# State chain of the recurrent heads: 64-column matmuls, one per head, in place of 128x128 products

## The chip, the cores and the metric

The kernel runs on one core of a Trainium2 chip. The metric is the device time of one execution in microseconds (us); lower is better. Times are given as the median of several runs. A core has TensorE (matmuls and weight loads), VectorE, ScalarE, GpSimd and SyncE (DMA issue), each with its own instruction queue; they meet at semaphores.

## The reference

One decoder layer over 512 tokens with 16 learned meta tokens ahead of them (528 in all), width 2048. After an RMS norm one projection feeds two groups of heads: 16 recurrent heads of 64 (RWKV-7) and 8 differential-attention heads. Both are gated, concatenated, projected, normed and added to the input. The change is in the recurrent heads:

```python
def step(S, inp):
    r_t, w_t, k_t, v_t, kk_t, b_t = inp
    sa = jnp.einsum('bhvk,bhk->bhv', S, -kk_t)
    S = S * w_t[:, :, None, :] + sa[..., None] * b_t[:, :, None, :] + v_t[..., None] * k_t[:, :, None, :]
    y = jnp.einsum('bhvk,bhk->bhv', S, r_t)
    return S, y
```

Each head carries a state S of 64x64 through all tokens; y is normed per head, a bonus term is added, and it is gated.

## The kernel before

The kernel is written engine by engine, with semaphores by hand. Two recurrent heads fill the 128 partitions and are called a pair; there are 8 pairs. The tokens are padded to 576 and cut into 9 chunks of 64 (`NC`), in 3 groups of 3 (`GC`, `NG`). The program runs through iterations: in iteration i TensorE computes the projection tiles of one pair or attention head (`feature_tile`, L547: three products of the split f32 operands for every 128 input features, 264 moving columns twice or 512 once), and between these matmuls it puts the work of the pair before. What stands where is a table of places by hand: each part of the work is a generator that yields the place of its next step, and `upto` runs the steps that are due between two projection matmuls. Nothing of the order is decided at run time; each engine's queue is fixed.

For each group `inv_pe` forms the triangular matrices of the three chunks (L646, by row halves, one matmul per head with 64 rows), inverts them in f16 (L667 to L701), and `chain_pe` then goes through the chunks one by one. With a chunk's two heads in one 128x128 array it makes five f32 products:

- g (L723): the chunk's keys times `home`, which holds on its diagonal quarters the two heads' states, and the values on the others. `home` is a 128x128 tile of `suv`, one for each chunk.
- first part of y (L725), from the same `home` with the queries; not in chunk 0.
- u (L728): the inverse `t_t` times g, once VectorE has copied g into `g_sb` (L1523). VectorE (L1528) and ScalarE (L1081) put the upper and the lower head's u into `home`.
- s (L733): the new state from `bk_tok` and `home`; not in the last chunk. VectorE scales it and adds the decayed old state that ScalarE prepared (L1538, L1075).
- second part of y (L736): from `home` and the masked matrix `b_in`; not in chunk 0. ScalarE copies y of a group to `ysum` (L1088).

So with 8 pairs there are 72 products g, 72 u, 64 s and 64 of each part of y, 336 in all. Products g, u and s use the PSUM columns 0 to 127 of `mb`, y those from 512 on. Of the blocks that g, u, s and the second y put out only the diagonal or a half is used: where the two heads' data lie side by side, the operands hold zeros or the result of the other quarters is left unread. The f32 matmul is executed in two passes, so the trace has two matmul and two weight-load records for each.

Other lines named below: L588, L592, L616 norms of the recurrent heads; L788 and L790 the product of attention with the values, where L790 has only the 16 rows of the meta tokens; L780 and L782 its transposes, L782 with 16 columns; L1055, L1059, L1062 ScalarE's and L1499 VectorE's copies in the inversion.

Of the kernel before, what the change touches and what calls it, by code (L numbers as in the profile page):

```python
# [34 lines left out]
P = 128  # L35
# [88 lines left out]
def hybrid_layer(nc, x, meta_tokens, pre_norm_w, w_in, rwkv_mu, rwkv_w0, rwkv_w_up, rwkv_a0, rwkv_a_up,  # L124
# [3 lines left out]
    with ctx:  # L128
# [40 lines left out]
        def carve(stage, name, n, dt=F32):  # L169
            at = taken.get(stage, 0)  # L170
            words = n if dt is F32 else n // 2
            taken[stage] = at + words
            assert taken[stage] <= ARENA, (stage, name, taken[stage])
            v = arena[:, at:at + words]
            return v if dt is F32 else v.bitcast(dt)
# [26 lines left out]
        b_in3 = [v.rearrange("p (c t) -> p c t", c=GC) for v in b_in]  # L202
        b_in5 = [v.rearrange("p (c k h t) -> p c k h t", c=GC, k=2, h=2) for v in b_in]
        state0 = carve("rwkv", "state0", HD)
        g_sb = carve("rwkv", "g_sb", P)
        top, bottom = slice(0, HD), slice(HD, P)
        halves = (top, bottom)

# [325 lines left out]
        def _(pe):  # L534
# [169 lines left out]
            def chain_pe(i, g, late, work, gn):  # L704
                b = g % 2
                n = groups_so_far(i, g, late)
                for c in range(GC):
                    ch = g * GC + c
                    m = chunks_so_far(i, ch, late)
                    home = suv[:, chunk_home(i, ch, late), :]  # L710
                    yield chain_at(g, 3 * c, late, work)
                    if c == 0:
                        pe.wait_ge(s("inv_taken"), n)
                        pe.wait_ge(s("k_masked"), 2 * n)
                        if g == 0:
                            pe.wait_ge(s("state_zeroed"), i)
                    if ch > 0:
                        pe.wait_ge(s("s_taken"), states_so_far(i, ch - 1, late))
                        if g > 0 and c == 0:
                            pe.wait_ge(s("y_taken"), n - 1)  # L720
                    o = mb[:, 0:P]
                    yo = mb[:, 512 + c * P:512 + (c + 1) * P]
                    mm(o, ar3[:, ch, 0:P], home, start=True, stop=True).then_inc(s("g_done"), 1)  # L723
                    if ch > 0:
                        mm(yo, home, ar3[:, ch, P:2 * P], start=True, stop=False)  # L725
                    yield chain_at(g, 3 * c + 1, late, work)
                    pe.wait_ge(s("g_taken"), m)
                    mm(o, t_t[b][:, c * P:(c + 1) * P], g_sb, start=True, stop=True).then_inc(s("u_done"), 1)  # L728
                    yield chain_at(g, 3 * c + 2, late, work)
                    pe.wait_ge(s("u_taken"), m)  # L730
                    pe.wait_ge(s("u_lower_taken"), m)
                    if ch < SC:
                        mm(o, bk_tok[g][:, c * P:(c + 1) * P], home, start=True,  # L733
                           stop=True).then_inc(s("s_done"), 1)
                    if ch > 0:
                        last = mm(yo, home, b_in3[g][:, c, P:2 * P], start=False, stop=True)  # L736
                        if c == GC - 1:
                            last.then_inc(s("y_done"), 1)

# [137 lines left out]
        def _(act):  # L877
# [186 lines left out]
            def chain_act(i, g, late, work, gn):  # L1064
                n = groups_so_far(i, g, late)
                for c in range(GC):
                    ch = g * GC + c
                    home = suv[:, chunk_home(i, ch, late), :]
                    yield chain_at(g, 3 * c + 0.3, late, work)
                    if 0 < ch < SC:  # L1070
                        act.wait_ge(s("s_taken"), states_so_far(i, ch - 1, late))
                        if ch == 1:
                            act.wait_ge(s("ends_made"), i - late)
                        for h, rows in enumerate(halves):
                            last = A(state0[rows, :], home[rows, rows], ACT.Copy, scale=w_end_of(i, late)[rows, ch:ch + 1])  # L1075
                        last.then_inc(s("s_scaled"), 1)
                    yield chain_at(g, 3 * c + 1.3, late, work)
                    if 0 < ch < SC:
                        act.wait_ge(s("s_scaled"), kept_so_far(i, ch, late))
                    act.wait_ge(s("u_done"), chunks_so_far(i, ch, late))  # L1080
                    A(home[bottom, bottom], mb[bottom, bottom], ACT.Copy).then_inc(s("u_lower_taken"), 1)  # L1081
                yield chain_at(g, 8.4, late, work)
                act.wait_ge(s("y_done"), n)
                c0 = 1 if g == 0 else 0
                lo, w = (g * GC + c0 - 1) * CH, (GC - c0) * CH
                y4 = mb[:, 512:512 + GC * P].rearrange("p (c h t) -> p c h t", c=GC, h=2)
                for h, rows in enumerate(halves):
                    last = A(ysum[rows, lo:lo + w].rearrange("p (c t) -> p c t", t=CH), y4[rows, c0:, h, :], ACT.Copy)  # L1088
                last.then_inc(s("y_taken"), 1)

            def attn_act(i, gn):
                n = i - NP_
# [143 lines left out]
        def _(dve):  # L1236
# [279 lines left out]
            def chain_dve(i, g, late, work, gn):  # L1516
                for c in range(GC):
                    ch = g * GC + c
                    m = chunks_so_far(i, ch, late)
                    home = suv[:, chunk_home(i, ch, late), :]  # L1520
                    yield chain_at(g, 3 * c + 0.3, late, work)
                    dve.wait_ge(s("g_done"), m)
                    V.tensor_copy(g_sb, mb[:, 0:P]).then_inc(s("g_taken"), 1)  # L1523
                    yield chain_at(g, 3 * c + 1.3, late, work)
                    dve.wait_ge(s("u_done"), m)
                    if 0 < ch < SC:
                        dve.wait_ge(s("s_scaled"), kept_so_far(i, ch, late))
                    V.tensor_copy(home[top, top], mb[top, top]).then_inc(s("u_taken"), 1)  # L1528
                    if ch < SC:
                        yield chain_at(g, 3 * c + 2.3, late, work)  # L1530
                        dve.wait_ge(s("s_done"), states_so_far(i, ch, late))
                        if ch == 0:
                            dve.wait_ge(s("ends_made"), i - late)
                        for rows in halves:
                            dst = suv[rows, chunk_home(i, ch + 1, late), rows]
                            src, w = mb[rows, rows], w_end_of(i, late)[rows, ch:ch + 1]
                            if ch:
                                ins = STT(dst, src, w, state0[rows, :], ALU.mult, ALU.add)  # L1538
                            else:
                                ins = TS(dst, src, w, None, ALU.mult)  # L1540
                        ins.then_inc(s("s_taken"), 1)
# [156 lines left out]
```

## Time and profile before

| what | us |
|---|---|
| median of 3 runs | 1394.71 |
| lowest and highest run | 1393.51 and 1394.75 |
| the profiled execution, its time | 1395.48 |
| the profiled execution, its span | 1393.7 |
| TensorE matmuls busy | 1329.2 |
| TensorE weight loads busy | 1136.1 |
| VectorE busy | 731.8 |
| ScalarE busy | 673.1 |
| GpSimd busy | 304.8 |

The profile lists busy time by engine: PE are TensorE's matmuls, PEld its weight loads, which overlap matmuls; DVE is VectorE, ACT ScalarE and POOL GpSimd. The time of a matmul runs from its start to its modelled end; matmuls are pipelined, so several are in flight and their durations add up to more than the time they take from the queue. That is read from one start to the next. The timeline view gives start and length in us, and merges instructions of the same line and shape that follow each other (x2 and so on); its first number plus its second is the end of the last of them. The waits view tells for how long an engine sat idle and which instruction let it go on.

### The profile page before, as it was taken

What the parts mean: (1) busy time and instruction counts of PE and PEld (TensorE: products, weight loads), DVE (VectorE), ACT (ScalarE), POOL (GpSimd) and SP (SyncE); (2) the same over time, 40 slices, a digit from 0 to 9 for tenths busy, and PEclk for the clock granted to TensorE, in tenths of its full rate; (3) what the DMA queues carried; (4) which work ended last, traced back from release to release, by engine and by line L of the source; (5) the groups of instructions that cost most, each with busy time, mean ns of one, the idle gap of its engine ahead of it and who ended that gap; (6) DMA issues with size and microseconds to landing.
All of it is one profiled execution on the core that took longest, in us unless ns stands there. A gap on an engine that the chain in (4) does not pass through costs nothing.

```text
span 1393.7 us, 24026 instructions
## 1 busy us (share of the span) xinstructions
PE 1329.2 (95%) x9393; PEld 1136.1 (82%) x9393; DVE 731.8 (53%) x1653; ACT 673.1 (48%) x1550; POOL 304.8 (22%) x234
## 2 busy tenths in 40 slices
PE   3999999999999999999999999999999999989997
PEld 3988888797888879889788877898888988768885
DVE  5346767767677686866866433433343333530013
ACT  4435656556565555656555544444443444432331
POOL 3330001000000100001000323333334333334544
PEclk9999999999999999999999998999999999999998
DMA  6221121111112111111112222222222222235333
GB/s 211 71 76 56 47 63 40 56 54 47 56 46 63 47 54 51 51 56 47 53 47 61 83 63 61 71 81 71 75 76 76 69 76 76 67 92 203 109 93 141
DMA packets 151264, 102.24 MB, mean 73 GB/s; under 512 B 6398, under 2 KB 140640, under 8 KB 149600
## 3 DMA queue, kind: packets, MB, share of 16 engines
q1 hardware_dynamic: 151152, 100.71, 24.3%
q8 instruction: 75, 1.23, 0.4%
q14 instruction: 37, 0.30, 0.1%
HBM read 96.49 MB, written 4.19 MB: 72 GB/s over the span
## 4 chain that ended last, share of the span: by engine, by line
PE 83%; DVE 9%; ACT 4%; issue 3%; POOL 1%; DMA 0%; DVEq 0%; ACTq 0%; SPq 0%
PE tile L547 48%; PE tile L807 2%; PE tile L808 2%; PE tile L809 2%; PE ma L773 2%; PE ma L646 2%; PE ma L686 1%; PE ma L679 1%; PE mb L788 1%; PE ma L667 1%; DVE arena L1499 1%; PE mb L790 1%; PE ma L809 1%; PE mb L807 1%; PE ma L807 1%
## 5 line engine op out<-in xcount | busy, mean ns | idle before, releaser
L547 PE MATMUL tile<-hn_hi,w_hi 128*128 128x264 f32 (+1 forms) x1696 | 446.6, 326 | 0.3
L547 PE MATMUL tile<-hn_hi,w_lo 128*128 128x264 f32 (+1 forms) x1696 | 438.6, 322 | 2.2 <-ACT arena L1062 2.2
L547 PE MATMUL tile<-hn_lo,w_hi 128*128 128x264 f32 (+1 forms) x1696 | 437.8, 321 | 0.0
L885 ACT CAST w_hi<-w_raw 128x512 fp32r<-128x512 f32 x324 | 200.4, 619 | 365.3 <-PE tile L547 254.9
L1177 POOL TENSOR_TENSOR w_lo<-w_raw,w_hi 128x512 fp32r<-128x512 f32 x196 | 255.1, 1302 | 448.3 <-ACT w_hi L885 448.2
L547 PEld LDWEIGHTS tile<-hn_hi,w_hi 128*128 128x128 f32 x1696 | 276.5, 190 | 29.2 <-issue 10.2
L547 PEld LDWEIGHTS tile<-hn_hi,w_lo 128*128 128x128 f32 x1696 | 276.3, 190 | 18.8 <-ACT arena L1062 3.6
L547 PEld LDWEIGHTS tile<-hn_lo,w_hi 128*128 128x128 f32 x1696 | 276.2, 190 | 11.6 <-issue 2.2
L1192 POOL TENSOR_TENSOR arena<-arena,power 128x10 f32<-128x10 f32 (+3 forms) x28 | 43.9, 1569 | 620.3 <-DVE arena L1356 471.2
L1499 DVE TENSOR_TENSOR arena<-ma,c 128x384 f16<-128x384 f32 x120 | 66.7, 556 | 45.9 <-PE ma L667 44.6
L1436 DVE TENSOR_TENSOR w_lo<-w_raw,w_hi 128x512 fp32r<-128x512 f32 x128 | 87.5, 683 | 1.3
L1059 ACT ACTIVATE arena<-ma 128x384 f16<-128x384 f32 x120 | 58.8, 490 | 46.3 <-PE ma L679 45.0
L1599 DVE TENSOR_SCALAR arena<-mb,arena 128x128 f32<-128x128 f32 x32 | 11.2, 350 | 91.9 <-PE mb L790 91.9
L807 PE MATMUL tile<-w_hi,hn_hi 128*128 128x512 f32 x128 | 53.1, 415 | 5.5 <-DVE hn_lo L1618 5.5
L1062 ACT ACTIVATE arena<-ma 128x384 f16<-128x384 f32 x120 | 58.3, 486 | 0.0
L808 PE MATMUL tile<-w_lo,hn_hi 128*128 128x512 f32 x128 | 51.6, 403 | 0.0
L809 PE MATMUL tile<-w_hi,hn_lo 128*128 128x512 f32 x128 | 51.5, 403 | 0.0
L1483 DVE TENSOR_TENSOR arena<-arena,c 128x384 f16<-128x384 f16 x144 | 49.0, 350 | 0.8
L1587 DVE TENSOR_TENSOR ma<-ma,c 128x128 f32<-128x128 f32 x32 | 9.6, 299 | 75.1 <-PE mb L773 75.1
L679 PE MATMUL ma<-arena 128*128 128x128 f16 x360 | 41.7, 224 | 3.3 <-DVE arena L1499 2.0
L667 PE MATMUL ma<-arena 128*128 128x128 f16 x360 | 41.6, 224 | 3.2 <-ACT arena L1059 3.1
L1075 ACT ACTIVATE arena<-arena 64x64 f32<-64x64 f32 x112 | 38.5, 344 | 12.0 <-DVE arena L1538 11.2
(262 smaller groups left out, 2090.1 us busy)
## 6 DMA issues: line engine op xcount, KB each, us to landing
w_raw<-w_in SPq DMA_DIRECT2D x260, 256.0 KB, 2.8
w_raw<-w_out SPq DMA_DIRECT2D x64, 256.0 KB, 3.0
big<-x SPq DMA_DIRECT2D x4, 1024.0 KB, 8.0
arena<-x SPq DMA_DIRECT2D x4, 1024.0 KB, 8.6
out<-big SPq DMA_DIRECT2D x3, 1024.0 KB, 3.9
arena<-post_norm_w SPq DMA_DIRECT2D x1, 1024.0 KB, 5.0
out<-big SPq DMA_DIRECT2D x2, 512.0 KB, 3.2
arena<-table_rope SPq DMA_DIRECT2D x2, 264.0 KB, 2.9
```

Of the source, the lines that this page charges most:

```text
L547: last = mm(o[:, at:at + n], w[:, slot, cols], t[:, kt, tok:tok + n], start=(kt == 0 and w is w_hi and t is hn_hi), stop=(kt == KT - 1 and ...
L667: last = mm(bank(0, c), bl(lv, (l - 1) * GC + c), bl(x16, c), start=True, stop=True)
L679: last = mm(bank(0, c), bl(xt16, c), bl(z16, c), start=True, stop=True)
L807: mm(banks[t], hn_hi[:, k, y], w_hi[:, k % RING, :], start=(k == 0), stop=False)
L808: mm(banks[t], hn_hi[:, k, y], w_lo[:, k % RING, :], start=False, stop=False)
L809: last = mm(banks[t], hn_lo[:, k, y], w_hi[:, k % RING, :], start=False, stop=(k == KT - 1))
L885: nc.scalar.copy(w_hi[:, slot, :], w_raw[:, slot, :]).then_inc(s("hi_done"), 1)
L1059: A(x16, ma[:, 0:W], ACT.Copy).then_inc(s("x_taken"), 1)
L1062: A(xt16, ma[:, 512:512 + W], ACT.Copy).then_inc(s("xt_taken"), 1)
L1177: T(w_lo[:, slot, :], w_raw[:, slot, :], w_hi[:, slot, :].bitcast(F32), ALU.subtract).then_inc(s("lo_done"), 1)
L1436: TT(w_lo[:, slot, :], w_raw[:, slot, :], w_hi[:, slot, :].bitcast(F32), ALU.subtract).then_inc(s("lo_done"), 1)
L1499: TT(g3(z16), g3(ma[:, 0:W]), every(ident16), ALU.add).then_inc(s("zz_taken"), 1)
```

## The change

Each of the five products becomes two matmuls with 64 output rows, one per head, the upper head's result in partitions 0 to 63 and the lower one's in 64 to 127, both in the same 64 PSUM columns. A matmul's weights are then 64 columns wide, and 64 columns move. For g, the first part of y and s the contraction still runs over 128 rows. For u and the second part of y it runs over the head's own 64 rows. A product's four passes (two per head) take the place of its two. The copies read 64 columns: `g_sb` is 64 wide, and `ysum` is filled by one copy of 128 partitions and not by two of 64.

```diff
@@ -202,7 +202,7 @@
         b_in3 = [v.rearrange("p (c t) -> p c t", c=GC) for v in b_in]
         b_in5 = [v.rearrange("p (c k h t) -> p c k h t", c=GC, k=2, h=2) for v in b_in]
         state0 = carve("rwkv", "state0", HD)
-        g_sb = carve("rwkv", "g_sb", P)
+        g_sb = carve("rwkv", "g_sb", CH)
         top, bottom = slice(0, HD), slice(HD, P)
         halves = (top, bottom)
 
@@ -718,22 +718,31 @@
                         pe.wait_ge(s("s_taken"), states_so_far(i, ch - 1, late))
                         if g > 0 and c == 0:
                             pe.wait_ge(s("y_taken"), n - 1)
-                    o = mb[:, 0:P]
-                    yo = mb[:, 512 + c * P:512 + (c + 1) * P]
-                    mm(o, ar3[:, ch, 0:P], home, start=True, stop=True).then_inc(s("g_done"), 1)
+                    o = mb[:, 0:CH]
+                    yo = mb[:, 512 + c * CH:512 + (c + 1) * CH]
+                    for rows in halves:
+                        last = mm(o[rows], ar3[:, ch, rows], home[:, rows], start=True, stop=True)
+                    last.then_inc(s("g_done"), 1)
                     if ch > 0:
-                        mm(yo, home, ar3[:, ch, P:2 * P], start=True, stop=False)
+                        for h, rows in enumerate(halves):
+                            mm(yo[rows], home[:, rows], ar5[:, ch, 1, h, :], start=True, stop=False)
                     yield chain_at(g, 3 * c + 1, late, work)
                     pe.wait_ge(s("g_taken"), m)
-                    mm(o, t_t[b][:, c * P:(c + 1) * P], g_sb, start=True, stop=True).then_inc(s("u_done"), 1)
+                    for h, rows in enumerate(halves):
+                        own = slice(c * P + h * CH, c * P + (h + 1) * CH)
+                        last = mm(o[rows], t_t[b][rows, own], g_sb[rows], start=True, stop=True)
+                    last.then_inc(s("u_done"), 1)
                     yield chain_at(g, 3 * c + 2, late, work)
                     pe.wait_ge(s("u_taken"), m)
                     pe.wait_ge(s("u_lower_taken"), m)
                     if ch < SC:
-                        mm(o, bk_tok[g][:, c * P:(c + 1) * P], home, start=True,
-                           stop=True).then_inc(s("s_done"), 1)
+                        for h, rows in enumerate(halves):
+                            dims = slice(c * P + h * HD, c * P + (h + 1) * HD)
+                            last = mm(o[rows], bk_tok[g][:, dims], home[:, rows], start=True, stop=True)
+                        last.then_inc(s("s_done"), 1)
                     if ch > 0:
-                        last = mm(yo, home, b_in3[g][:, c, P:2 * P], start=False, stop=True)
+                        for h, rows in enumerate(halves):
+                            last = mm(yo[rows], home[rows, rows], b_in5[g][rows, c, 1, h, :], start=False, stop=True)
                         if c == GC - 1:
                             last.then_inc(s("y_done"), 1)
 
@@ -1078,15 +1087,12 @@
                     if 0 < ch < SC:
                         act.wait_ge(s("s_scaled"), kept_so_far(i, ch, late))
                     act.wait_ge(s("u_done"), chunks_so_far(i, ch, late))
-                    A(home[bottom, bottom], mb[bottom, bottom], ACT.Copy).then_inc(s("u_lower_taken"), 1)
+                    A(home[bottom, bottom], mb[bottom, 0:CH], ACT.Copy).then_inc(s("u_lower_taken"), 1)
                 yield chain_at(g, 8.4, late, work)
                 act.wait_ge(s("y_done"), n)
                 c0 = 1 if g == 0 else 0
                 lo, w = (g * GC + c0 - 1) * CH, (GC - c0) * CH
-                y4 = mb[:, 512:512 + GC * P].rearrange("p (c h t) -> p c h t", c=GC, h=2)
-                for h, rows in enumerate(halves):
-                    last = A(ysum[rows, lo:lo + w].rearrange("p (c t) -> p c t", t=CH), y4[rows, c0:, h, :], ACT.Copy)
-                last.then_inc(s("y_taken"), 1)
+                A(ysum[:, lo:lo + w], mb[:, 512 + c0 * CH:512 + GC * CH], ACT.Copy).then_inc(s("y_taken"), 1)
 
             def attn_act(i, gn):
                 n = i - NP_
@@ -1520,12 +1526,12 @@
                     home = suv[:, chunk_home(i, ch, late), :]
                     yield chain_at(g, 3 * c + 0.3, late, work)
                     dve.wait_ge(s("g_done"), m)
-                    V.tensor_copy(g_sb, mb[:, 0:P]).then_inc(s("g_taken"), 1)
+                    V.tensor_copy(g_sb, mb[:, 0:CH]).then_inc(s("g_taken"), 1)
                     yield chain_at(g, 3 * c + 1.3, late, work)
                     dve.wait_ge(s("u_done"), m)
                     if 0 < ch < SC:
                         dve.wait_ge(s("s_scaled"), kept_so_far(i, ch, late))
-                    V.tensor_copy(home[top, top], mb[top, top]).then_inc(s("u_taken"), 1)
+                    V.tensor_copy(home[top, top], mb[top, 0:CH]).then_inc(s("u_taken"), 1)
                     if ch < SC:
                         yield chain_at(g, 3 * c + 2.3, late, work)
                         dve.wait_ge(s("s_done"), states_so_far(i, ch, late))
@@ -1533,7 +1539,7 @@
                             dve.wait_ge(s("ends_made"), i - late)
                         for rows in halves:
                             dst = suv[rows, chunk_home(i, ch + 1, late), rows]
-                            src, w = mb[rows, rows], w_end_of(i, late)[rows, ch:ch + 1]
+                            src, w = mb[rows, 0:CH], w_end_of(i, late)[rows, ch:ch + 1]
                             if ch:
                                 ins = STT(dst, src, w, state0[rows, :], ALU.mult, ALU.add)
                             else:
```

The order of the steps stays. In the middle of the program, from one chunk of the chain to the next, TensorE's queue has this before; L733 is s, L736 the second part of y, L723 g and L725 the first part of y:

```order
L547 MATMUL tile<-hn_lo,w_hi 128x264 x2
L547 MATMUL tile<-hn_hi,w_lo 128x264 x2
L733 MATMUL mb<-arena 128x128
L736 MATMUL mb<-arena 128x128
L547 MATMUL tile<-hn_hi,w_hi 128x264 x2
L547 MATMUL tile<-hn_lo,w_hi 128x264 x2
L667 MATMUL ma<-arena 128x128 x3
L674 MATMUL ma<-c,xv 128x128 x2
L547 MATMUL tile<-hn_hi,w_lo 128x264 x2
L547 MATMUL tile<-hn_hi,w_hi 128x264 x2
L723 MATMUL mb<-arena 128x128
L725 MATMUL mb<-arena 128x128
```

After the change L741 is s, L745 the second part of y, L724 g and L728 the first part of y (u, which was L728, is L733). The shape is that of the output:

```order
L547 MATMUL tile<-hn_lo,w_hi 128x264 x2
L547 MATMUL tile<-hn_hi,w_lo 128x264 x2
L741 MATMUL mb<-arena 64x64 x2
L745 MATMUL mb<-arena 64x64 x2
L547 MATMUL tile<-hn_hi,w_hi 128x264 x2
L547 MATMUL tile<-hn_lo,w_hi 128x264 x2
L667 MATMUL ma<-arena 128x128 x3
L674 MATMUL ma<-c,xv 128x128 x2
L547 MATMUL tile<-hn_hi,w_lo 128x264 x2
L547 MATMUL tile<-hn_hi,w_hi 128x264 x2
L724 MATMUL mb<-arena 64x64 x2
L728 MATMUL mb<-arena 64x64 x2
```

Every product has kept its place between the same projection matmuls and is two instructions instead of one. In front of a group and behind it stand matmuls with all 128 rows and columns, at all but 8 places.

## Rows read from the trace of the kernel before

**Rows 1.** The page's first part: engine, busy us, share of span, instructions.
```profile
PE 1329.2 (95%) x9393; PEld 1136.1 (82%) x9393; DVE 731.8 (53%) x1653; ACT 673.1 (48%) x1550; POOL 304.8 (22%) x234
```

**Rows 2.** Busy times in a stretch: us, PE, PEld, DVE, ACT, POOL, clock, DMA, GB/s.
```profile
90.00:775.00 685.00, 667.28 (x5555) 575.75 (x5554) 484.73 (x1119) 385.22 (x916) 32.83 (x20) 1.00 0.19 54
```

**Rows 3.** Waits of PE, 90 to 775 us: total us, times, longest us.
```profile
PE ma L686 <- ACT arena L1055: 3.9, 8, 0.9
...
PE mb L728 <- DVE arena L1523: 3.0, 8, 0.4
...
PE mb L723 <- DVE arena L1538: 0.5, 1, 0.5
```

**Rows 4.** Groups by line and shape, PE: count | busy us, mean ns | idle.
```profile
L723 PE MATMUL mb<-arena 128*128 128x128 f32 x144 | 29.2, 284 | 1.1 <-DVE arena L1538 0.5
...
L588 PE MATMUL tile<-arena,c 128*128 128x512 f32 x14 | 7.2, 592 | 0.0
...
L592 PE MATMUL tile<-c,tanh_g 128*128 128x2 f32 x56 | 6.6, 240 | 0.0
```

**Rows 5.** Timeline of PE and PEld, 401.0 to 403.3 us: start, length, line.
```profile
401.77 0.40 PE L547 MATMUL tile<-hn_hi,w_hi 128*128 128x264 f32 x2
...
402.75 0.38 PE L728 MATMUL mb<-arena 128*128 128x128 f32 x2
...
402.01 0.17 PEld L667 LDWEIGHTS ma<-arena 128*128 128x128 f16 x3
...
402.62 0.32 PEld L728 LDWEIGHTS mb<-arena 128*128 128x128 f32 x2
402.86 0.30 PEld L547 LDWEIGHTS tile<-hn_hi,w_hi 128*128 128x128 f32 x2
```

**Rows 6.** The same, 810.8 to 812.4 us.
```profile
810.87 0.41 PE L547 MATMUL tile<-hn_hi,w_lo 128*128 128x264 f32 x2
811.11 0.61 PE L788 MATMUL mb<-arena 128*128 128x128 f32 x4
811.64 0.48 PE L790 MATMUL mb<-arena 16*128 16x128 f32 x2
812.06 0.51 PE L547 MATMUL tile<-hn_hi,w_hi 128*128 128x264 f32 x2
...
811.64 0.29 PEld L790 LDWEIGHTS mb<-arena 16*128 16x128 f32 x2
812.06 0.30 PEld L547 LDWEIGHTS tile<-hn_hi,w_hi 128*128 128x128 f32 x2
```

**Rows 7.** The same, 127.5 to 129.2 us.
```profile
127.58 0.41 PE L547 MATMUL tile<-hn_hi,w_lo 128*128 128x264 f32 x2
127.92 0.94 PE L646 MATMUL ma<-arena 64*128 64x128 f32 x12
128.78 0.51 PE L547 MATMUL tile<-hn_hi,w_hi 128*128 128x264 f32 x2
...
127.91 0.75 PEld L646 LDWEIGHTS ma<-arena 64*128 64x128 f32 x12
128.78 0.30 PEld L547 LDWEIGHTS tile<-hn_hi,w_hi 128*128 128x128 f32 x2
```

**Rows 8.** The same, 819.3 to 820.4 us.
```profile
819.65 0.49 PE L780 MATMUL ma<-c,arena 128*128 128x128 f32 x3
819.98 0.27 PE L782 MATMUL ma<-c,arena 128*16 128x128 f32 x1
...
819.87 0.09 PEld L782 LDWEIGHTS ma<-c,arena 128*16 128x16 f32 x1
819.98 0.19 PEld L547 LDWEIGHTS tile<-hn_hi,w_hi 128*128 128x128 f32 x1
```

**Rows 9.** Groups by line and shape, VectorE's copies in the chain.
```profile
L1523 DVE COPY arena<-mb 128x128 f32<-128x128 f32 x72 | 20.8, 288 | 34.8 <-PE mb L723 33.7
...
L1528 DVE COPY arena<-mb 64x64 f32<-64x64 f32 x72 | 15.3, 213 | 15.3 <-PE mb L728 15.1
```

## The prediction

> **What bounds the kernel now.** I read the engine shares first: TensorE has a matmul in flight for 1329.2 of 1393.7 us [rows 1], so what an edit adds to TensorE's queue or takes out of it is the first term. The state chain is spread over the stretch from 90 to 775 us, where matmuls fill 667.28 of 685.00 us at the full granted clock (1.00, that is 2.4 GHz) [rows 2]. The waits of that stretch come next: time in which TensorE has no matmul and waits for ScalarE or VectorE is seven rows from 3.9 us down to 0.5 us, 15.2 us in all; of these the chain's own copy L1523 ends 3.0 us [rows 3]. So the chain is mostly hidden between projection matmuls (L547), and its price is the TensorE time it takes.
>
> What a matmul costs there isn't its listed duration (0.28 us for one of L723 [rows 4]) but the step to the next. An f32 product is two passes of one instruction each (L723: 72 products, 144 matmuls). Two passes of L728 take from 402.62 to 402.86 on the weight-load row, 0.12 each with the wait for the wider L547 in front; in the run of four L788 passes it is 0.11 [rows 5, 6]. The reader should see there that the next weight load starts at 402.86 while L728 ends at 402.75 + 0.38 = 403.13: **loads run 0.27 us ahead of the end of the matmul before**, and so are hidden.
>
> Now the stretches where the number of rows changes. L790 uses 16 rows behind L788 with 128: L788 ends at 811.11 + 0.61 = 811.72 and the load of L790 starts at 811.64, 0.08 before the end. Back again, L790 ends at 812.12 and the load of L547 starts at 812.06 [rows 6]. The same at L646, which works in row halves: 127.99 against 127.91 on the way in, and 128.86 against 128.78 on the way out [rows 7]. **The array runs empty at each change.** The price by whole stretches: from the end of L547 before (811.28) to the end of the L547 pair behind (812.57) is 1.29 us, and at full pace its passes would take 4 x 0.11 + 2 x 0.11 + 2 x 0.12 = 0.90; so 0.39 for two changes. At L646 it is 129.29 - 127.99 = 1.30, less six steps of two passes at once (0.107 each) and 2 x 0.12 = 0.88; so 0.42. I take 0.20 for one change. L646 shows a gain too: its twelve passes take six steps, since row halves load and stream side by side.
>
> The Trainium skill has this as a rule (TensorEngine Tiling, Key Properties): changing the tiling mode, and not just the tile, drains the engine. The trace agrees for rows, 0.20 us a time.
>
> **The change part by part.** One product of two passes becomes two matmuls of two passes, 64 columns of weights and 64 moving columns each. For a 64-column pass: an f32 pass lasts 0.59 us with 512 moving columns [rows 4] and 0.27 us with 128 (L782) [rows 8], so 0.83 ns a column and 0.054 us for 64. With 2 moving columns the weight load of 128 columns alone sets the pace (6.6 us of matmul rows for 56 is 0.118 each); half of the 0.107 that a load shows in L646 is 0.054 too [rows 4, 7]. So a pass of 64 by 64 steps at 0.054 if the two heads go side by side, and at 0.11 for the pair if they go one after the other.
>
> (a) The second and fifth products (u, 72 times; the part of y from the inputs, 64 times) also split the contraction: head h uses rows and columns of its own half. That is a change of rows in front and one behind, 136 times. In front: 0.20 less the 0.053 that the shorter exposed load saves = 0.145. Behind: 0.20. Passes: 2 x 0.054 = 0.11 in place of 0.22. Together +0.145 + 0.20 - 0.11 = +0.23; **136 x 0.23 = +31 us**. This rests on rows alone.
>
> (b) The other three (g 72, first part of y 64, s 64: 200 products) keep 128 rows and split columns. No row shows column halves. Side by side each saves 0.22 - 0.11 = 0.11, 200 x 0.11 = -22 us; but where L547 follows (72 groups of g and y, 8 s without y) its 128-column load is longer than the last short pass and shows by 0.053, 80 x 0.053 = +4. Sum **-18 us**. One after the other it would be 0 + 4 = +4 us. I take -18, since the two row halves of L646 do run side by side [rows 7].
>
> The Trainium skill says the same of narrow outputs (TensorE: Matmul & The Clock Gate, Part 3): small M placed at distinct column groups runs concurrently, 2.38 times faster for three; no run here shows it.
>
> (c) Does going from 128x128 to column halves also empty the array? Bounds: nothing, or what rows cost. The nearest row for nothing is L782, whose weights are 16 columns wide: L780 ends at 820.14 and the load of L782 starts at 819.87, 0.27 before; behind it L782 ends at 820.25 and L547 loads from 819.98 [rows 8]. No cost, but L782 is a transpose that takes one pass, not two, and sits in the first columns; it needn't have been set up as a column tile. For a cost speak all row changes, wide and narrow, in both directions. Price: 136 entries (72 groups of g, 64 of s) x 0.145 = 19.7, and 80 exits x (0.20 - 0.053) = 11.8; **+31 us**. A middle is shown by L547 to the f16 L667: load at 402.01, the matmul before it ends at 402.17, so 0.16 ahead rather than 0.27 or 0.08 [rows 5]; an entry then shows 0.057 more than now (-0.16 + 0.054 + 0.217 for the short load and the short pass, less 0.054), an exit 0.05, and 136 x 0.057 + 80 x 0.05 = +12 us.
>
> For (c) the Trainium skill speaks twice against this change: the rule above names the mode as such, and the page's Restrictions say that column tiling disables transpose mode for FP32, by which L782 was no column tile and shows nothing. By the rule the sum has the +31, by L782 it has 0. I take the +31, since a drain at each of the row changes shows that the array doesn't overlap two layouts.
>
> (d) VectorE and ScalarE: L1523 copies 64 columns, not 128. It takes 0.29 us, a 64x64 copy 0.21 [rows 9], so 72 x 0.08 = 6 us less work; it ends TensorE's wait 8 times [rows 3], so under 1 us of it is on the path. ysum is one copy for two. Both engines have room, so nothing is booked.
>
> (e) Absorbed: TensorE waits 15.2 us for the other two there [rows 3]; a wait shrinks when TensorE comes later, unless what it waits for was itself fed by TensorE. Bounds 0 and 15; I take half, -8 us, since there are some two array changes from one wait to the next.
>
> Sum: 31 - 18 + 31 - 8 = **+36 us**. The profiled execution took 1395.48 us with a span of 1393.7; the median of the three runs is 1394.71, 0.8 below it. Added to the median: **1431 us**.
>
> **Rivals.**
> *Column changes are free.* L782 speaks for it, the row changes against. 31 - 18 - 4 (less delay, less absorbed) = +9: 1404 us.
> *In between.* Free changes but heads one after the other (31 + 4 - 8 = +27: 1422), or the middle price of (c) (31 - 18 + 12 - 6 = +19: 1414).
> *Both bad.* Columns drain and nothing goes side by side: 31 + 4 + 31 - 10 = +56: 1451 us.
> *Faster: the drains fall into the waits.* Place: the 90 to 775 us stretch, where TensorE's order is fixed and VectorE is late at L728, L679, L686. If column changes are free, the net cost is 31 - 18 = 13 us, against 15.2 us of waits [rows 3]. It turns at 13 absorbed, and all 15.2 absorbed with the shorter L1523 (-1) gives -3: 1392 us. Against it: drains lie in all 136 places, waits in some 40.
> *The change doesn't do what it says*: the split products might run in one layout without row changes. Then only the widths count, -22 to 0: 1373 to 1395. The L646 rows, which are split the same way by operand slices, speak against it.
>
> **How the numbers follow.** Columns drain (forecast) 0.46; free 0.24; in between 0.16; both bad 0.06; faster or absorbed 0.08. The forecast's case alone spans 1422 to 1440. For 8 in 10 the range takes in "free" and "in between" from 1400 and goes to 1445; it leaves out "both bad" and "faster". A measurement of this kernel can't tell less than 0.2% (2.8 us). Faster by more than that 0.05, within 0.06, slower 0.89.
>
> **What would show it.** In the new trace: at u and the last part of y, load starts 0.08 before the end of the matmul in front, and again at the L547 behind (a); the two heads' passes at the same start (b); at g and s the lead of the load, 0.08 for a drain, 0.27 for none (c); fewer and shorter TensorE waits for L1499, L1055 and the g copy (e). The forecast is wrong if the lead at g is 0.27 (near 1404), or if the two heads' 64x64 passes don't start together, or if the granted clock of the stretch falls below 1.00 from a less filled array, which no term has.

## The result: 2.4% slower, at the forecast's own layout prices

| | before | after |
|---|---|---|
| median, us | 1394.11 | 1425.99 |
| lowest to highest run, us | 1393.46 to 1394.75 | 1424.41 to 1431.52 |
| the profiled execution, its time and span, us | 1395.48, 1393.7 | 1424.41, 1422.6 |

The ratio is 1.0237, with a 95% interval of 1.0214 to 1.0259: +31.9 us by the medians, where +36 was forecast. One execution further down, of extra4_cols, took 2656.72 us against 1449.54 to 1450.11 for its three others, and is left out of its median.

The engine shares of after, as [rows 1]:

```profile
PE 1366.6 (96%) x10065; PEld 1121.4 (79%) x10065; DVE 729.5 (51%) x1653; ACT 666.6 (47%) x1526; POOL 304.8 (21%) x234
```

TensorE's rows grew by 37.4 us while its count grew by 672 matmuls. The stretch that [rows 2] shows for before now ends some 25 to 30 us later; this is its row (us, PE, PEld, DVE, ACT, POOL, granted clock, DMA, GB/s):

```profile
90.00:805.00 715.00, 706.04 (x6215) 562.81 (x6215) 481.00 (x1117) 379.28 (x892) 33.12 (x20) 1.00 0.18 52
```

Now the three kinds of places: what is read is the lead, the time by which the next weight load (PEld) starts before the modelled end of the matmul in front. It was 0.27 us where the layout stays and 0.08 where the number of rows changes. Timelines of after, TensorE's matmuls and loads, start and length in us; first g (L724) with the first part of y (L728), behind two L547 passes of 264 columns:

```profile
404.24 0.41 PE L547 MATMUL tile<-hn_lo,w_hi 128*128 128x264 f32 x2
404.57 0.34 PE L724 MATMUL mb<-arena 128*64 128x64 f32 x4
404.74 0.29 PE L728 MATMUL mb<-arena 128*64 128x64 f32 x4
...
404.57 0.20 PEld L724 LDWEIGHTS mb<-arena 128*64 128x64 f32 x4
404.68 0.20 PEld L728 LDWEIGHTS mb<-arena 128*64 128x64 f32 x4
404.95 0.19 PEld L547 LDWEIGHTS tile<-hn_hi,w_lo 128*128 128x128 f32 x1
```

L547 ends at 404.24 + 0.41 = 404.65 and the load of g starts at 404.57, 0.08 before: the short lead of [rows 6, 7]. All 128 rows are in use here, so **a change to column halves costs the same**. From g to y there is no change: L724 ends at 404.91, L728 loads from 404.68, 0.23 ahead. And the eight passes take 0.46 us, from 404.57 to the end of L728 at 405.03: one load (0.05), three steps of 0.05 to 0.06 from one pair of passes to the next, and the length of the last pass (0.22). Seven such steps, one head after the other, would need over 0.6. In the trace the two passes of a pair start 7 ns apart. **The two heads go side by side.** Back to 128 columns there is a change again, 405.03 against 404.95.

u (L733), 64 rows and 64 columns, has one on each side: 406.62 against 406.54, and 406.88 against 406.81.

```profile
406.22 0.40 PE L547 MATMUL tile<-hn_hi,w_lo 128*128 128x264 f32 x2
406.55 0.33 PE L733 MATMUL mb<-arena 64*64 64x64 f32 x4
...
406.54 0.20 PEld L733 LDWEIGHTS mb<-arena 64*64 64x64 f32 x4
406.81 0.30 PEld L547 LDWEIGHTS tile<-hn_hi,w_hi 128*128 128x128 f32 x2
```

s (L741) and the second part of y (L745): between the two as well, 410.15 against 410.07, and behind, 410.40 against 410.33.

```profile
409.81 0.34 PE L741 MATMUL mb<-arena 128*64 128x64 f32 x4
410.07 0.33 PE L745 MATMUL mb<-arena 64*64 64x64 f32 x4
...
410.07 0.19 PEld L745 LDWEIGHTS mb<-arena 64*64 64x64 f32 x4
410.33 0.19 PEld L547 LDWEIGHTS tile<-hn_lo,w_hi 128*128 128x128 f32 x1
```

The whole trace of after shows it, not only these places. Where the layout changes and no wait for VectorE stands in front, the lead is 0.07 us at every one of them (0.08 by the rounded numbers above): into and out of the groups of g, at u, into s, between s and the second part of y (56 of 56), and behind. From g to y it is 0.22 or more at all 64.

The trace gives the price too: the time from the start of the second matmul ahead of a group to the start of the third behind it, after less before, by the median. It is 0.23 us for u (71 places), 0.13 for g with the first part of y (62), 0.28 for s with the second part of y (55), and 0.23 to 0.24 where one product stands alone (8 places of each kind). Times their number that is 46 us, where (a) to (c) of the prediction booked 44.

The waits of TensorE's matmuls for other engines (total us, times, longest us), as [rows 3]. They were 15.2 us, to 775 us, and are 6.2, to 805 us, where the same work ends; u's wait for the copy of g fell from 3.0 to 1.4 us:

```profile
PE ma L686 <- ACT arena L1064: 2.9, 8, 0.9
PE mb L733 <- DVE arena L1529: 1.4, 7, 0.2
PE ma L679 <- DVE arena L1505: 0.6, 1, 0.6
...
PE ma L667 <- ACT arena L1068: 0.4, 1, 0.4
```

The weight-load rows show more waits, since a load can wait while a matmul is still in flight. Before, in the same stretch to 805 us, the six largest waits for ScalarE and VectorE were 39.6 us in all:

```profile
PEld ma L679 <- DVE arena L1499: 11.3, 23, 0.8
...
PEld ma L667 <- ACT arena L1059: 6.6, 16, 0.6
...
PEld mb L728 <- DVE arena L1523: 6.2, 8, 0.8
PEld ma L686 <- ACT arena L1055: 5.5, 9, 1.0
PEld tile L547 <- ACT arena L1062: 5.5, 17, 0.5
...
PEld mb L723 <- DVE arena L1538: 4.5, 9, 0.6
```

After, the same six places (L1505 is what was L1499, L1064 was L1055, L1068 was L1059, L1071 was L1062; L733 behind L1529 is u, L724 behind L1544 is g) hold 27.0 us:

```profile
PEld ma L679 <- DVE arena L1505: 8.1, 17, 0.8
...
PEld ma L686 <- ACT arena L1064: 4.5, 9, 1.0
PEld mb L733 <- DVE arena L1529: 4.4, 7, 0.6
PEld tile L547 <- ACT arena L1071: 3.6, 17, 0.2
PEld ma L667 <- ACT arena L1068: 3.3, 10, 0.6
...
PEld mb L724 <- DVE arena L1544: 3.1, 8, 0.6
```

The copy of g became shorter, 288 to 222 ns [rows 9]:

```profile
L1529 DVE COPY arena<-mb 128x64 f32<-128x64 f32 x72 | 16.0, 222 | 40.9 <-PE mb L724 40.4
```

### The profile page after: what moved, and what is told of

Read it like the earlier page. It is cut to its first block, busy times and chain, and to the rows that moved or that the text cites. A ratio compares the mean times of both kernels' runs of the same rounds, so it can differ in the third digit from the quotient of the medians.

```text
span 1422.6 us, 25346 instructions
## 1 busy us (share of the span) xinstructions
PE 1366.6 (96%) x10065; PEld 1121.4 (79%) x10065; DVE 729.5 (51%) x1653; ACT 666.6 (47%) x1526; POOL 304.8 (21%) x234
## 4 chain that ended last, share of the span: by engine, by line
PE 87%; DVE 6%; ACT 3%; issue 2%; POOL 1%; DMA 0%; DVEq 0%; ACTq 0%; SPq 0%
PE tile L547 52%; PE tile L816 2%; PE tile L817 2%; PE tile L818 2%; PE ma L782 2%; PE ma L686 1%; PE ma L646 1%; PE ma L667 1%; PE ma L679 1%; PE mb L733 1%; PE mb L797 1%; PE mb L745 1%; PE mb L724 1%; PE mb L741 1%; PE mb L799 1%
## 5 line engine op out<-in xcount | busy, mean ns | idle before, releaser
L547 PE MATMUL tile<-hn_hi,w_hi 128*128 128x264 f32 (+1 forms) x1696 | 447.2, 326 | 0.3
L547 PE MATMUL tile<-hn_hi,w_lo 128*128 128x264 f32 (+1 forms) x1696 | 439.3, 322 | 0.3
L547 PE MATMUL tile<-hn_lo,w_hi 128*128 128x264 f32 (+1 forms) x1696 | 439.3, 322 | 0.0
L547 PEld LDWEIGHTS tile<-hn_hi,w_hi 128*128 128x128 f32 x1696 | 275.7, 189 | 33.2 <-issue 10.2
L547 PEld LDWEIGHTS tile<-hn_hi,w_lo 128*128 128x128 f32 x1696 | 275.5, 189 | 21.2 <-issue 3.4
L547 PEld LDWEIGHTS tile<-hn_lo,w_hi 128*128 128x128 f32 x1696 | 275.4, 189 | 17.2 <-issue 2.2
L1505 DVE TENSOR_TENSOR arena<-ma,c 128x384 f16<-128x384 f32 x120 | 66.7, 556 | 59.0 <-PE ma L667 58.0
L1068 ACT ACTIVATE arena<-ma 128x384 f16<-128x384 f32 x120 | 58.7, 490 | 53.7 <-PE ma L679 52.8
L1071 ACT ACTIVATE arena<-ma 128x384 f16<-128x384 f32 x120 | 58.2, 485 | 0.0
```

The lines of the kernel that those rows point to most:

```text
L547: last = mm(o[:, at:at + n], w[:, slot, cols], t[:, kt, tok:tok + n], start=(kt == 0 and w is w_hi and t is hn_hi), stop=(kt == KT - 1 and ...
L1068: A(x16, ma[:, 0:W], ACT.Copy).then_inc(s("x_taken"), 1)
L1071: A(xt16, ma[:, 512:512 + W], ACT.Copy).then_inc(s("xt_taken"), 1)
L1505: TT(g3(z16), g3(ma[:, 0:W]), every(ident16), ALU.add).then_inc(s("zz_taken"), 1)
```

## The experiments

All are compared by the medians of runs on the same chip; the kernel before took 1393.19, 1394.00 and 1393.24 us in the three sets, and each run is compared with its own. Because the work of an iteration repeats exactly, the trace gives a second, finer reading: when the last matmul of a fixed line starts. For the recurrent stretch it is L622, once in each of the iterations 0 to 7 (by the products g between the first and the last of them, 6.2 of the 8 chains of nine chunks lie there).

**Which products cost what.** From the kernel before, one step at a time is split.

only_u:

```diff
-mm(o, t_t[b][:, c * P:(c + 1) * P], g_sb, start=True, stop=True).then_inc(s("u_done"), 1)
+for h, rows in enumerate(halves):
+    own = slice(c * P + h * CH, c * P + (h + 1) * CH)
+    last = mm(o[rows, rows], t_t[b][rows, own], g_sb[rows, rows], start=True, stop=True)
+last.then_inc(s("u_done"), 1)
```

> The kernel before, with u alone split by rows and columns (72 products); all others 128x128. Theory (each change of the array's layout lets it run empty): 72 places, each -0.22 + 2 x 0.05 for the passes and 0.145 + 0.20 for two changes, 16.3 us before anything is absorbed; TensorE's other waits shrink and take about a third, so about +11 us, 1405 us, and the load of L547 behind u starts after a gap. Rival (nothing is absorbed, and what was missing of the sum is the granted clock): +16 us, 1410 us.

only_g:

```diff
-mm(o, ar3[:, ch, 0:P], home, start=True, stop=True).then_inc(s("g_done"), 1)
+for rows in halves:
+    last = mm(o[rows, 0:CH], ar3[:, ch, rows], home[:, rows], start=True, stop=True)
+last.then_inc(s("g_done"), 1)
...
-mm(o, t_t[b][:, c * P:(c + 1) * P], g_sb, start=True, stop=True).then_inc(s("u_done"), 1)
+mm(o[:, 0:CH], t_t[b][:, c * P:(c + 1) * P], g_sb, start=True, stop=True).then_inc(s("u_done"), 1)
```

> The kernel before, with g alone split by columns, all 128 rows kept; u is then one product with 128 weight columns and 64 moving ones, the copies of g and u read 64 columns. First part of y, s and second part of y stay 128x128. Theory (column halves are a layout of their own, and a change to them costs what a change of rows costs): 72 places, each 0.20 (entry) + 0.05 + 0.31 (exit to a 128-column load) in place of 0.33, +0.23 each, 16 us, less a third absorbed and a shorter copy: +10 us, 1404 us. Rival (only a change in the number of rows costs, the g group paid for its neighbours in the queue): two heads side by side save, -0.06 x 72 = -4 us, 1390 us.

only_s_y2:

```diff
-mm(o, bk_tok[g][:, c * P:(c + 1) * P], home, start=True, stop=True).then_inc(s("s_done"), 1)
+for h, rows in enumerate(halves):
+    dims = slice(c * P + h * HD, c * P + (h + 1) * HD)
+    last = mm(o[rows, rows], bk_tok[g][:, dims], home[:, rows], start=True, stop=True)
...
-last = mm(yo, home, b_in3[g][:, c, P:2 * P], start=False, stop=True)
+for h, rows in enumerate(halves):
+    last = mm(yo[rows, rows], home[rows, rows], b_in5[g][rows, c, 1, h, :], start=False, stop=True)
```

> The kernel before, with s (columns) and the second part of y (rows and columns) split, 64 products each; g, first part of y and u stay 128x128. Theory: 56 places with both cost 0.82 in place of 0.57, 16 places with one of them 0.23 each: 14.2 + 3.7 = 18 us, less a third absorbed: +12 us, 1406 us. Rival (nothing absorbed): +18 us, 1412 us.

| kernel | median, us | ratio, 95% interval | over before | booked before absorption |
|---|---|---|---|---|
| only_u | 1405.68 | 1.0082, 1.0067 to 1.0097 | +12.5 | +16 |
| only_g | 1400.44 | 1.0047, 1.0032 to 1.0062 | +7.3 | +16 |
| only_s_y2 | 1411.91 | 1.0126, 1.0111 to 1.0141 | +18.7 | +18 |

L622 (shortest, median and longest in ns, then first to last start in us), of before, after, only_u, only_g and only_s_y2, one row each in this order:

```profile
L622 PE MATMUL tile<-lora,arena x32: 589/641/693, 79.0 to 653.3; 64*128 64x512 f32 x32
```

```profile
L622 PE MATMUL tile<-lora,arena x32: 589/693/1219, 79.3 to 677.5; 64*128 64x512 f32 x32
```

```profile
L622 PE MATMUL tile<-lora,arena x32: 589/641/693, 79.4 to 662.1; 64*128 64x512 f32 x32
```

```profile
L622 PE MATMUL tile<-lora,arena x32: 589/641/693, 79.4 to 658.4; 64*128 64x512 f32 x32
```

```profile
L622 PE MATMUL tile<-lora,arena x32: 589/693/1219, 79.5 to 666.4; 64*128 64x512 f32 x32
```

From first to last it is 574.3 us before and 598.2 after (+23.9), 582.7 (+8.4), 579.0 (+4.7) and 586.9 (+12.6, of which 1.7 are a stretch of lower clock, see the end). only_g settles the question of (c): g alone, with all rows kept and two heads side by side, makes the kernel slower, where the rival wanted 1390. only_u came as booked less a quarter. The other two show that "a third is absorbed" is no constant: of g's 16 us more than half vanished (its copies also got shorter, and its gaps stand right ahead of the places where TensorE waits), of s and y hardly anything. By its median only_s_y2 fits the reading without absorption; by L622, 12.6 - 1.7 = 10.9 for 6.2 of 8 chains, so 14 for all, it lies between.

What is missing can be set beside the waits that became shorter, as their views have them for each of these kernels:

| kernel | booked less measured, us | fall of the matmul waits | fall of the load waits at the six places |
|---|---|---|---|
| only_u | 3.8 | 3.5 | 3.5 |
| only_g | 8.7 | 6.1 | 6.9 |
| only_s_y2 | -0.7, 1.0 without its lower clock | 2.8 | 3.9 |
| after | 12.1, 13.8 without its lower clock | 9.0 | 12.6 |

So shorter waits are about what is missing for u, g and the whole change, and the load rows come nearer; s with the second part of y fits neither. The three kernels together cost 38.5 us; the first part of y, which rides with g and was not run alone, was booked at 64 x 0.11 = 7 us less, and 31.5 is within 0.4 us of the whole change: nothing is seen of one product's price depending on another.

**Is it rows, or any layout?** rows_128 is the changed kernel with all ten matmuls as column halves:

```diff
-last = mm(o[rows], t_t[b][rows, own], g_sb[rows], start=True, stop=True)
+last = mm(o[rows], t_t[b][:, own], g_sb, start=True, stop=True)
...
-last = mm(yo[rows], home[rows, rows], b_in5[g][rows, c, 1, h, :], start=False, stop=True)
+last = mm(yo[rows], home[:, rows], b_in5[g][:, c, 1, h, :], start=False, stop=True)
```

> The changed kernel, but u and the second part of y contract over all 128 rows (the other head's rows meet zeros), so that all ten matmuls of a chunk are column halves and none splits rows. Theory (a change of layout costs, whichever it is): u costs what it did, and between s and the second part of y there is no change left: 56 x 0.145 = 8 us less than the changed kernel, some of it given back by waits: 1420 us. Rival (row changes are the dear ones): 136 x 0.23 less, about 1400 us. Second rival (it is the number of instructions): no difference, 1426 us.

It took 1416.06 us, ratio 1.0165 (1.0148 to 1.0182): 9.9 less than after, and 9.0 less when each is set against its own set's before. The rivals wanted 26 or 0. L622:

```profile
L622 PE MATMUL tile<-lora,arena x32: 589/641/693, 78.8 to 670.5; 64*128 64x512 f32 x32
```

591.7 us is 6.5 below after, and without after's clock stretch 4.8, so 6.2 for all chains. So the one change taken out (between s and y, 56 times) is worth 6 to 9 us. Its trace shows the two places, s with y and then u:

```profile
406.94 0.34 PE L741 MATMUL mb<-arena 128*64 128x64 f32 x4
...
411.44 0.41 PE L547 MATMUL tile<-hn_hi,w_lo 128*128 128x264 f32 x2
...
407.05 0.20 PEld L745 LDWEIGHTS mb<-arena 128*64 128x64 f32 x4
...
411.78 0.20 PEld L733 LDWEIGHTS mb<-arena 128*64 128x64 f32 x4
```

L741 ends at 407.28 and L745 loads 0.23 before: no change. L547 ends at 411.85 and u loads 0.07 before: the change at u is still paid, with all 128 rows in use.

u_whole puts u back to one product, with 64 moving columns:

```diff
-for h, rows in enumerate(halves):
-    own = slice(c * P + h * CH, c * P + (h + 1) * CH)
-    last = mm(o[rows], t_t[b][rows, own], g_sb[rows], start=True, stop=True)
-last.then_inc(s("u_done"), 1)
+mm(o, t_t[b][:, c * P:(c + 1) * P], g_sb, start=True, stop=True).then_inc(s("u_done"), 1)
```

> The changed kernel, but u is one product: 128x128 weights, 64 moving columns, result in the same 64 columns. Theory: its passes are bound by the weight load (0.11 each), both changes around it go, 72 x 0.23 = 16 us less before absorption, about 11 us net: 1415 us. Rival (with all others split, u's changes were hidden): 1426 us.

1413.42 us, ratio 1.0140 (1.0123 to 1.0156), 12.6 below after: u costs the same alone (+12.5) as among the others.

**Do two heads go side by side?** twice_after issues g twice:

```diff
-for rows in halves:
-    last = mm(o[rows], ar3[:, ch, rows], home[:, rows], start=True, stop=True)
+for again in range(2):
+    for rows in halves:
+        last = mm(o[rows], ar3[:, ch, rows], home[:, rows], start=True, stop=True)
```

> The changed kernel with g issued twice, the second overwriting the first with the same values: two more column-half matmuls in a layout that is already set. Theory (two heads go side by side): two steps of 0.05, 72 x 0.11 = 7.5 us before absorption, and at most that: 1430 to 1434 us. Rival (one head after the other): 72 x 0.21 = 15 us: 1437 to 1441 us.

1430.85 us, ratio 1.0264 (1.0249 to 1.0280): +4.9 over after for 72 products, 0.07 us each, where one after the other needs 0.21. Side by side, as the timeline above shows.

**The price where nothing waits.** In the attention iterations 10 to 15 TensorE hardly waits (two matmul waits, 3.2 and 0.7 us, as long with the added pairs as before). There 72 places got added matmuls whose result nobody reads, between projection matmuls, into the projection's other PSUM tile:

```diff
+if part == 1 and spare is not None:
+    for rows in halves:
+        mm(spare[rows, 0:CH], ident[rows, rows], c32v("block")[rows, rows], start=True, stop=True)
```

> The kernel before with 72 added pairs of f32 matmuls that nobody reads: 64 rows, 64 weight columns, 64 moving, one for each half, the shape of the split u. They stand between projection matmuls of the attention iterations (860 to 1200 us), 12 in each of six, where TensorE waits for nobody. Theory: no wait can take anything up there, so the full price shows, 0.20 + 0.05 + 0.32 - 0.12 = 0.45 each, 32 us: 1426 us, and 16 us above extra_whole. Rival (the price of a change depends on the recurrent stretch): another difference to extra_whole.

extra_cols has `ident[:, rows]` and `c32v("block")[:, rows]` in it, extra_whole one `mm(spare[:, 0:P], ident, c32v("block"), ...)`; extra4_cols and extra4_whole do the same four times over, into columns of their own.

> As extra_halves (72 added pairs in the attention iterations, results unread), but each matmul of a pair uses all 128 rows and 64 weight columns: column halves alone. Theory (a change to column halves costs what a change of rows costs): 0.44 each as in extra_halves (5.3 us for an iteration of 12), 1426 us. Rival (columns cost less than rows): between that and the 0.20 of extra_whole.

> The same 72 added places, each one f32 product of 128x128 (two passes) in one layout with its neighbours. Theory: 0.11 + 0.11 each and no gap, 16 us: 1410 us.

> As extra_cols, with four column-half products in a row at each of the 72 places. Theory (one price at the way in and out, 0.05 a step between): 0.20 + 7 x 0.052 + 0.32 - 0.12 = 0.76 each, 9.2 us for an iteration, 1449 us, and less than extra4_whole. Rival (each product pays): 4 x 0.44 = 1.8 each, over 1500 us.

> Four whole 128x128 f32 products at each of the same 72 places (results unread). Theory: 0.20 for the first, 0.22 for each more, 0.87, 10.4 us for an iteration, 1456 us, 7 to 8 us above extra4_cols.

The attention product (L788 before) starts first and last in these kernels at, in the order before, extra_halves, extra_cols, extra_whole, extra4_cols, extra4_whole:

```profile
L788 PE MATMUL mb<-arena x160: 270/275/422, 800.3 to 1238.9; 128*128 128x128 f32 x160
```

```profile
L791 PE MATMUL mb<-arena x160: 270/275/377, 799.5 to 1268.9; 128*128 128x128 f32 x160
```

```profile
L791 PE MATMUL mb<-arena x160: 270/275/377, 799.0 to 1267.8; 128*128 128x128 f32 x160
```

```profile
L790 PE MATMUL mb<-arena x160: 270/275/377, 799.7 to 1251.4; 128*128 128x128 f32 x160
```

```profile
L793 PE MATMUL mb<-arena x160: 270/275/377, 799.0 to 1291.9; 128*128 128x128 f32 x160
```

```profile
L791 PE MATMUL mb<-arena x160: 270/275/377, 799.9 to 1300.0; 128*128 128x128 f32 x160
```

| kernel | median, us | over before | per place | booked |
|---|---|---|---|---|
| extra_halves | 1425.51 | +31.5 | 0.44 | 0.45 |
| extra_cols | 1425.80 | +32.6 | 0.45 | 0.44 |
| extra_whole | 1408.55 | +14.6 | 0.20 | 0.22 |
| extra4_cols | 1449.88 | +56.6 | 0.79 | 0.76 |
| extra4_whole | 1457.04 | +63.8 | 0.89 | 0.87 |

Per place is the rise by 72. The L788 rows say the same: from first to last they span 438.6 us before, 469.4 and 468.8 with halves, 451.7 with whole products, 492.9 and 500.1 with four of each; halves less whole is 17.7, four halves less four whole -7.2 us; the stretches of lower clock in these six executions differ, which can shift such a difference by 2 to 3 us. The first two show the full price: 0.24 more than the whole product, and 72 x 0.24 = 17 us for what cost 12.5 in the recurrent stretch (only_u). Of the 4 to 5 us that are missing there, 3.5 are seen as shorter waits (table above); the clock can't be the reason, since only_u has no lower clock in that stretch. Rows and columns, or columns alone: the same. And the price is one for the run and not for each product: **four products in a row are 7 us cheaper as halves** than whole. The number of instructions isn't the price either: four in a row have 16 passes as halves and 8 whole.

**Taking changes out.** If that is right, the kernel before pays it too, at the 32 products over the 16 meta tokens (L790) [rows 6]. meta_full_rows lets them run over 128 rows, the added ones zero:

```diff
-mm(o, attn_t[0:META, 4 * P:5 * P], vt[0:META, m * P:(m + 1) * P], start=False,
+mm(o, attn_t[:, 4 * P:5 * P], vt[:, m * P:(m + 1) * P], start=False,
...
+V.memset(attn_t[:, 4 * P:5 * P], 0.0)
+V.memset(vt[:, 4 * P:5 * P], 0.0)
```

> The kernel before, with the 32 products of attention and values for the 16 meta tokens (L790) run over all 128 rows: rows 16 to 127 of the weights are zeros, set once by VectorE. It takes away 64 changes of layout between 790 and 1240 us and changes nothing else. Theory: 0.39 x 32 = 12.5 us less, all of it, since TensorE waits for nobody there: 1382 us, 0.9% faster than the kernel before. Rival (those gaps come from the few rows or from a wait, not from the change of layout): 1394 us.

**1383.32 us, ratio 0.9929 (0.9915 to 0.9942)**, 9.9 us less than before and faster than both kernels. Its timeline at the place that [rows 6] shows of before:

```profile
809.87 0.60 PE L788 MATMUL mb<-arena 128*128 128x128 f32 x4
810.31 0.39 PE L790 MATMUL mb<-arena 128*128 128x128 f32 x2
810.45 0.49 PE L547 MATMUL tile<-hn_hi,w_hi 128*128 128x264 f32 x2
...
810.20 0.30 PEld L790 LDWEIGHTS mb<-arena 128*128 128x128 f32 x2
810.42 0.30 PEld L547 LDWEIGHTS tile<-hn_hi,w_hi 128*128 128x128 f32 x2
```

L788 ends at 810.47 and the load of L790 starts at 810.20, 0.27 ahead; L547 loads at 810.42, 0.28 before L790's end. From L788's first pass to the end of the L547 pair it is 810.94 - 809.87 = 1.07 us, before 812.57 - 811.11 = 1.46. That is the 0.39 expected at this place. First to last start of L788:

```profile
L788 PE MATMUL mb<-arena x160: 270/275/377, 799.4 to 1226.3; 128*128 128x128 f32 x160
```

426.9 us against 438.6, 11.7 less, but part of it is before's longer fall of the clock at 825 us (shown at the end). By the starts of the matmuls around each L790, 31 of the 32 places became 0.38 to 0.40 us shorter, and one more, with before's fall of the clock in it: 0.39 x 32 = 12.5, as expected. But once in an iteration the transpose behind the last of its four products (L796) waits for VectorE, and TensorE, being earlier, now waits longer. The load waits there in six iterations, before and now:

```profile
PEld ma L796 <- DVE arena L1608: 2.0, 6, 0.4
```

```profile
PEld ma L796 <- DVE arena L1610: 3.2, 6, 0.6
```

That is 0.2 us more in an iteration, 1.6 in eight, and leaves 10.9 us of the 12.5; the medians have 9.9.

## Why the prediction was right, and where its terms were off

The bound was read rightly: TensorE's queue is the price, and the layout changes are its largest part. (a) to (c) booked 44 us, and the places in the trace of after show 46.

(a) u and the second part of y: the leads of 0.08 on both sides are there, the passes of both heads step together. only_u and u_whole give 12.5 for u, extra_halves 17 us where next to nothing waits, booked was 72 x 0.23 = 16.6.

(b) Two heads side by side: right, by the timeline, twice_after (+4.9 for at most 7.5) and extra4_cols.

(c) The open question, and the one that carried the chance of 0.46: column halves are a layout like any other. Of the two neighbours in the trace of before the row changes were the right one, and L782, a transpose with 16 weight columns, was not; no run here shows why it keeps its lead of 0.27. So the +31 was a choice between two neighbours, held at less than even chances, and the runs bear it out. only_g, rows_128 and extra_cols each show it. By the Trainium skill (TensorEngine Tiling, Key Properties) changing the mode drains the engine; the trace now agrees for columns too, with 0.08 us of lead at L724 and 0.24 us over the whole product in extra_cols. The middle price (+12) needed a lead of 0.16 and is refuted, and so are the heads one after the other.

(d) 66 ns less for each copy of g where 80 were booked, 4.8 us of VectorE's time and not 6; only_g suggests that it counted for more than "under 1 us", but no run separates it.

(e) is the term that was mis-sized. Booked was -8 us out of 15.2 us of matmul waits. The 44 booked in (a) to (c) came out as 31.9, so 12 us were absorbed; by the 46 of the trace 14, and two more if the 1.7 us of lower clock, which no term has, are taken out. That is nearer to the bound of 15.2 than to its half. The matmul waits, the view that the term was sized from, fell by 9.0 us, the load waits at the six places by 12.6, from 39.6. So the load rows account for more of what is missing, and the likely reason is that a late load costs time even while the matmul ahead is still in flight; no run separates this from what the shorter copies of g gave. With 8 in place of 12 the sum came out 4 us high.

The rival "faster" needed 13 of 15 us absorbed at a net cost of 13; the absorbed 12 us and more came, but against 44. "The change doesn't do what it says" is out by the timelines.

## What to carry to other kernels

In this kernel a matmul or a run of them in another layout than its neighbours (16 or 64 of 128 rows, or 64 of 128 columns) cost about 0.35 us beside its passes for the way in and the way out together with 64 weight columns, and 0.39 to 0.42 with 128. The transpose L782 with 16 columns showed no such price. Splitting an f32 product into halves that run side by side gives 0.11 us of it back. So look at the run and not at the product: here one halved product between 128x128 ones lost 0.24 us, two in one layout 0.13, and four in a row won 0.10 (0.79 against 0.89 us). The same reading pays in reverse: the 16-row products amid full ones became cheaper when they were padded with zeros to the full shape, which was worth 0.7% of this kernel. What a slower TensorE gets back from waits is better sized from the waits of the weight loads than of the matmuls; here a third of them went, 12.6 of 39.6 us, which is one kernel's figure and a guess elsewhere.

## What the runs showed of the hardware beside this

The granted clock fell to its lower level once in the recurrent stretch of after, where before has none, though matmul rows fill 24.87 of 25 us (columns as above, the clock is the third from the right):

```profile
400.00:425.00 25.00, 24.87 (x223) 20.34 (x222) 15.56 (x36) 14.39 (x33) 1.95 (x1) 0.93 0.13 38
```

Before, the same stretch and the one at 825 us, where it has its longest fall:

```profile
400.00:425.00 25.00, 24.30 (x194) 19.59 (x194) 20.81 (x45) 16.48 (x37) 0.00 (x0) 1.00 0.19 54
825.00:850.00 25.00, 19.36 (x86) 14.56 (x85) 9.49 (x22) 7.33 (x18) 5.91 (x5) 0.80 0.15 43
```

0.93 over 25 us is 3.5 us at the lower level (1.2 in place of 2.4 GHz), which costs 1.7 us. In the recurrent stretch only_s_y2, u_whole and twice_after show one such fall each, only_u, only_g and rows_128 none. What brings it about is open. The spread of after, from 1424.41 us (mean granted clock 0.992) to 1431.52 (0.986), when before stays within 1.3 us, goes with the clock too.
